# The DSA indexer of a decoder step, written out: keys of four batches turned before their products, products issued over four column strips, the sums one chunk later, all key copies on VectorE, and ScalarE left to issue loads

## The reference, cut to what matters

```python
s = jnp.einsum('bqhi,bki->bqhk', iq, ik)                              # iq: 8 x 8 tokens, 4 heads, 64 wide; ik: 8 x 4104 keys, 64 wide
score = jnp.einsum('bqhk,bqh->bqk', jax.nn.relu(s), iw)               # a weighted sum of 4 heads
score = jnp.where(causal[None], score, -jnp.inf)
vals, idx = lax.top_k(score, top)                                     # 256 keys for each query, taken later
```

## Time and profile before

| what | value |
|---|---|
| time, median of 3 runs | 3029.92 us (3025.42 to 3032.97) |
| the profiled execution, its own time | 3023.38 us |
| its span, first to last instruction | 3021.5 us |
| the stage of `index_scores`, first load to last instruction | 1377.2 to 1516.1 us |
| one chunk of the stage, from the fourth on | 15.12 us |
| granted TensorE clock over the span | 0.907 |

### The profile page before, as it was taken

One profiled execution on the slowest core, in us unless ns is written; L12 is line 12 of the kernel. 1 busy time (PEld: TensorE's weight loads), 2 busy tenths in 40 slices (PEclk: granted clock), 3 DMA queues, 4 the chain that ended last, 5 costly groups with the idle time before them and its releaser, 6 DMA issues. The chain is left out here.

```text
span 3021.5 us, 45203 instructions
## 1 busy us (share of the span) xinstructions
PE 2406.0 (80%) x16080; PEld 1792.4 (59%) x16080; DVE 1041.9 (34%) x1834; ACT 757.9 (25%) x1700; POOL 494.9 (16%) x338
## 2 busy tenths in 40 slices
PE   4799999999948888836858868888499453677996
PEld 2688888888838888832335534444255342555885
DVE  3211111010002221302248846766233259655413
ACT  2000000000012222210135434454255253344000
POOL 4533333333240000000000000000000000132431
PEclk9999999999979999967979978989799775898998
DMA  2523233232376363672289889999699460001323
GB/s 82 171 99 115 99 108 105 100 114 85 150 204 216 124 209 114 213 176 64 48 264 354 298 319 381 377 375 333 198 380 340 154 215 0 1 1 69 99 84 111
DMA packets 306803, 524.96 MB, mean 174 GB/s; under 512 B 63373, under 2 KB 80030, under 8 KB 304174
## 3 DMA queue, kind: packets, MB, share of 16 engines
q1 hardware_dynamic: 272442, 486.57, 47.2%
q10 hardware_dynamic: 31648, 31.64, 3.5%
q0 software_dynamic: 2560, 4.80, 0.5%
HBM read 500.65 MB, written 44.00 MB: 180 GB/s over the span
## 5 line engine op out<-in xcount | busy, mean ns | idle before, releaser
L422 PE MATMUL proj_acc<-proj_w_hi,h_hi 128*128 128x512 f32 (+1 forms) x960 | 370.0, 385 | 16.6 <-POOL proj_w_lo L391 16.6
L423 PE MATMUL proj_acc<-proj_w_hi,h_lo 128*128 128x512 f32 (+1 forms) x960 | 370.1, 386 | 0.0
L424 PE MATMUL proj_acc<-proj_w_lo,h_hi 128*128 128x512 f32 (+1 forms) x960 | 369.6, 385 | 0.0
L391 POOL TENSOR_TENSOR proj_w_lo<-proj_w,proj_w_hi 128x2048 fp32r<-128x2048 f32 (+1 forms) x60 | 272.0, 4534 | 476.2 <-DVE proj_w_hi L360 476.2
L360 DVE CAST proj_w_hi<-proj_w 128x2048 fp32r<-128x2048 f32 (+1 forms) x60 | 80.6, 1345 | 483.6 <-PE proj_acc L415 461.8
L664 PE MATMUL cmp_hp<-cmp_xT,cmp_w 128*128 128x128 f32 x2048 | 230.0, 275 | 0.0
L664 PEld LDWEIGHTS cmp_hp<-cmp_xT,cmp_w 128*128 128x128 f32 x2048 | 229.3, 192 | 0.0
L1186 PE MATMUL sb_tp<-kept_consts,sb_k_rows 128*128 128x128 f32 x1024 | 170.0, 316 | 64.1 <-DMA sb_k_rows<-in_cache_sb_kv_dram 47.1
L422 PEld LDWEIGHTS proj_acc<-proj_w_hi,h_hi 128*128 128x128 f32 x960 | 180.8, 188 | 52.7 <-issue 17.1
L446 ACT COPY proj_out<-proj_acc 128x512 f32<-128x512 f32 (+1 forms) x60 | 34.7, 579 | 705.6 <-PE proj_acc L424 705.6
L1186 PEld LDWEIGHTS sb_tp<-kept_consts,sb_k_rows 128*128 128x128 f32 x1024 | 127.2, 159 | 138.6 <-ACT sb_kT L1326 63.7
(11 more groups left out here) (398 smaller groups left out, 3599.7 us busy)
## 6 DMA issues: line engine op xcount, KB each, us to landing
cmp_rows<-in_cache_nsa_kv_dram SPq DMA_DIRECT2D x256, 256.0 KB, 5.2
slc_rows<-in_cache_nsa_kv_dram SPq DMA_DIRECT2D x256, 256.0 KB, 5.0
sb_k_rows<-in_cache_sb_kv_dram SPq DMA_DIRECT2D x256, 256.0 KB, 5.9
sb_v_rows<-in_cache_sb_kv_dram SPq DMA_DIRECT2D x256, 256.0 KB, 7.3
dsa_rows<-in_cache_dsa_kv_dram SPq DMA_DIRECT2D x256, 256.0 KB, 4.9
proj_w<-in_w_in_dram SPq DMA_DIRECT2D x56, 1024.0 KB
fin_w<-in_w_out_dram SPq DMA_DIRECT2D x32, 512.0 KB
proj<-proj_out ACTq DMA_DIRECT2D x14, 1024.0 KB, 4.4
```

The lines of the kernel that those rows point to most:

```text
L391: pool.tensor_tensor(w_lo[q][:, :, 0:width], w[q][:, :, 0:width], w_hi[q][:, :, 0:width], ALU.subtract).then_inc(lo_made, 1)
L422: pe.matmul(to, h_hi[:, kk, r], w_hi[q][:, k, 0:width], start=(kk == 0), stop=False)
L423: pe.matmul(to, h_lo[:, kk, r], w_hi[q][:, k, 0:width], start=False, stop=False)
L424: last = pe.matmul(to, h_hi[:, kk, r], w_lo[q][:, k, 0:width], start=False, stop=(kk == KT_IN - 1))
```

## The change

Only `index_scores` is changed. Its arithmetic is the same.

- Three sets of `rows` instead of two (BUF), four `tp` instead of two (TB), eight `kT` (one for each batch) instead of two.
- PE: the keys of batches 0 to 3 are turned, then the sums of the chunk before are taken, then batches 4 and 5 are turned, then the products of batches 0 to 3 are issued, then 6 and 7 are turned, then the products of 4 to 7. Within a group the first half of all four strips comes ahead of the second half. One semaphore increment for four products.
- DVE makes all eight key copies of a chunk. It weighs group 0 after them, and group 1 after the first two copies of the next chunk.
- ACT issues the loads of a chunk, and from the fourth chunk on copies the `total` of three chunks before behind them.
- All loops are written out.

```diff
-        rows = [s.sb(f"rows{i}", [P, NB, PPC, 64]) for i in range(2)]
-        kT = [s.sb(f"kT{i}", [P, 2, P]) for i in range(2)]
+        BUF, TB = 3, 4
+        rows = [s.sb(f"rows{i}", [P, NB, PPC, 64]) for i in range(BUF)]
+        kT = [s.sb(f"kT{b}", [P, 2, P]) for b in range(NB)]
-        tp = [s.ps(f"tp{i}", [P, 2, P]) for i in range(2)]
+        tp = [s.ps(f"tp{i}", [P, 2, P]) for i in range(TB)]
...
+        def load(eng, engine, first, c):
+
+            pages = page_numbers(nc, io, kept.by_chunk, (c * NB + first) * PPC, 4 * PPC, engine)
+            for b in range(first, first + 4):
+                if c >= BUF:
+                    eng.wait_ge(turned, (c - BUF) * NB + b + 1)
+                load_pages(eng, pages[(b - first) * PPC:(b - first + 1) * PPC], rows[c % BUF][:, b], io.idx_cache, 0, 64, rows_in[c % BUF][b])
 
         @block.sync
         def _(sp):
...
+            for c in range(NCH):
+                load(sp, mybir.EngineType.SP, 0, c)
 
         @block.tensor
         def _(pe):
...
+            def turn(c, b):
+                n = c * NB + b
+                pe.wait_ge(rows_in[c % BUF][b], 64 * (c // BUF) + 64)
+                if n >= TB:
+
+                    pe.wait_ge(copied, n - TB + 1)
+                for q in range(2):
+                    last = pe.transpose(tp[n % TB][:, q, :], rows[c % BUF][:, b, 2 * q:2 * q + 2, :].rearrange("p a d -> p (a d)"), kept.ident)
+                last.then_inc(turned, 1)
+
+            def products(c, g):
+                if c:
+                    pe.wait_ge(weighted, (c - 1) * 2 + g + 1)
+                pe.wait_ge(copied, c * NB + 4 * g + 4)
                 for half in range(2):
-                    to = sp_[g][32 * r:32 * r + 32, :].rearrange("p (q a k) -> p a q k", a=2, k=P)[:, half]
-                    last = pe.matmul(to, kept.q_idx[:, half, b, :], kT[b % 2][:], start=(half == 0), stop=(half == 1),
-                                     tile_position=(0, 32 * r), skip_group_check=True)
+                    for r in range(4):
+                        to = sp_[g][32 * r:32 * r + 32, :].rearrange("p (q a k) -> p a q k", a=2, k=P)[:, half]
+                        last = pe.matmul(to, kept.q_idx[:, half, 4 * g + r, :], kT[4 * g + r][:], start=(half == 0), stop=(half == 1),
+                                         tile_position=(0, 32 * r), skip_group_check=True)
                 last.then_inc(multiplied, 1)
...
+            def add_up(c, width):
+                if c:
+                    pe.wait_ge(total_copied, c)
+                for g in range(2):
+                    pe.wait_ge(weighted, c * 2 + g + 1)
+                    pe.matmul(total[:, 0:width], seli[g], relu[g][:, 0:width], start=(g == 0), stop=(g == 1)).then_inc(summed, 1)
+
+            for c in range(NCH):
+                for b in range(4):
+                    turn(c, b)
+                if c:
+                    add_up(c - 1, CH)
+                for b in range(4, 6):
+                    turn(c, b)
+                products(c, 0)
+                for b in range(6, NB):
+                    turn(c, b)
+                products(c, 1)
+            add_up(NCH - 1, CH)
...
         @block.vector
         def _(dve):
...
+            def copy_keys(c, b):
+                dve.wait_ge(turned, c * NB + b + 1)
+                if c:
+
+                    dve.wait_ge(multiplied, (c - 1) * 2 + b // 4 + 1)
+                dve.tensor_copy(kT[b][:], tp[(c * NB + b) % TB][:]).then_inc(copied, 1)
+
+            def weigh(c, g, width):
+                dve.wait_ge(multiplied, c * 2 + g + 1)
+                if c:
+                    dve.wait_ge(summed, (c - 1) * 2 + g + 1)
...
+            for c in range(NCH):
                 for b in range(NB):
-                    if b % 2 == 0:
-                        copy_keys(dve, c * NB + b, b)
-                    if b == 5:
-                        weigh(0, c, CH)
-                weigh(1, c, CH)
...
+                    copy_keys(c, b)
+                    if b == 1 and c:
+                        weigh(c - 1, 1, CH)
+                weigh(c, 0, CH)
+            weigh(NCH - 1, 1, CH)
+            weigh(NCH, 0, NT)
+            weigh(NCH, 1, NT)
...
         @block.scalar
         def _(act):
...
+            def take_total(c):
+                act.wait_ge(summed, c * 2 + 2)
+                act.copy(kept.scores[:, c * CH:(c + 1) * CH], total[:]).then_inc(total_copied, 1)
+
+            for c in range(NCH):
+                load(act, mybir.EngineType.Activation, 4, c)
+                if c >= BUF:
+                    take_total(c - BUF)
+            for c in range(NCH - BUF, NCH):
+                take_total(c)
```

More of the change, by code:

```diff
@@ L823, in index_scores @@
         sp_ = [s.ps(f"sc{g}", [P, CH]) for g in range(2)]
         total = s.ps("total", [NS, CH])
-        rows_in = [[s.sem(f"rows_in{i}_{b}") for b in range(NB)] for i in range(2)]
-        turned, even_copied, odd_copied, multiplied = s.sem("turned"), s.sem("even_copied"), s.sem("odd_copied"), s.sem("multiplied")
+        rows_in = [[s.sem(f"rows_in{i}_{b}") for b in range(NB)] for i in range(BUF)]
+        turned, copied, multiplied = s.sem("turned"), s.sem("copied"), s.sem("multiplied")
         weighted, summed, total_copied, masked = s.sem("weighted"), s.sem("summed"), s.sem("total_copied"), s.sem("masked")
-        copied_by = (even_copied, odd_copied)
@@ L842, in _ @@
         @block.sync
         def _(sp):
[L844 to L848, removed]
+            for c in range(NCH):
+                load(sp, mybir.EngineType.SP, 0, c)
         @block.tensor
         def _(pe):
-            pe.nop().then_inc(turned, 2 * NB)
-            pe.nop().then_inc(multiplied, 2)
@@ L855, in product @@
-            def product(b, n):
-                g, r = divmod(b, 4)
-                pe.wait_ge(copied_by[b % 2], n + 2)
+            def turn(c, b):
[6 more added lines that the diff above has]
+                last.then_inc(turned, 1)
@@ L895, in _ @@
+            add_up(NCH - 1, CH)
             for g in range(2):
-                pe.wait_ge(weighted, NCH * 2 + g + 1)
+                pe.wait_ge(weighted, (NCH - 1) * 2 + g + 1)
                 for r in range(4):
@@ L900, in _ @@
                                      start=True, stop=True, tile_position=(0, 32 * r))
[L901 to L912, removed]
+                last.then_inc(multiplied, 1)
@@ L914, in _ @@
+            add_up(NCH, NT)
         @block.vector
         def _(dve):
[L916 to L922, removed]
+            def copy_keys(c, b):
[3 more added lines that the diff above has]
+                dve.tensor_copy(kT[b][:], tp[(c * NB + b) % TB][:]).then_inc(copied, 1)
@@ L923, in weigh @@
+            def weigh(c, g, width):
+                dve.wait_ge(multiplied, c * 2 + g + 1)
+                if c:
+                    dve.wait_ge(summed, (c - 1) * 2 + g + 1)
                 dve.tensor_scalar(relu[g][:, 0:width], sp_[g][:, 0:width], 0.0, kept.w_idx[:, g:g + 1], ALU.max, ALU.mult).then_inc(weighted, 1)
-            with dve.Fori(0, NCH) as c:
+            for c in range(NCH):
                 for b in range(NB):
-                    if b % 2 == 0:
-                        copy_keys(dve, c * NB + b, b)
-                    if b == 5:
-                        weigh(0, c, CH)
-                weigh(1, c, CH)
@@ L932, in _ @@
-            weigh(0, NCH, NT)
-            weigh(1, NCH, NT)
-            dve.wait_ge(summed, 2 * NCH + 2 + 2)
+                    copy_keys(c, b)
[5 more added lines that the diff above has]
+            weigh(NCH, 1, NT)
+            dve.wait_ge(summed, 2 * NCH + 2)
             dve.tensor_tensor(kept.scores[:, PAST:KEYS], total[:, 0:NT], kept.consts[0:NS, C_NM:C_NM + NT], ALU.add).then_inc(masked, 1)
```

## The result

The changed kernel takes 2985.68 us (median of 4 runs, 2982.61 to 2989.57) against 3028.54 for the kernel before in the same measurement (4 runs). The ratio is 0.986, 95% interval 0.9847 to 0.9874, a gain of 42.9 us. A second measurement on another occasion gave 0.9865 (0.9843 to 0.9887). The forecast was 2984.

What follows compares the result with a forecast made beforehand. PE's order of work bounded most of the stage; after the change, load issues would. Issues ending at 1453.1 plus a 16.8 us end gave 1469.9 instead of 1516.1, so 3029.9 - 46 = 2984 us, range 2976 to 3004.

Steps and rivals of the forecast that it cites:

- The place: The `index_scores` stage overlaps neither neighbour, so its shortening from 138.9 us, 46.2 us, reaches the kernel's total whole.
- The sign that would have spoken against it: The next stage, `slc_sample`, lengthening after its earlier start; it was forecast to keep its length.
- PE's chunk: PE's work per chunk in `index_scores` falls from 15.1 to 7.0 us, with four products overlapping on four strips.
- the wait for the last copy: PE's second product group waits 0.6 us a chunk for DVE's key copy of batch 7.
- The loads as the bound: SP's and ACT's load issues, 9.5 us a chunk, exceed PE's 7.0 and set the stage's pace.
- The term for irregular issues: Extra time in the load lists: chunk 0's 0.4 us excess over chunk 1, put down three more times.
- The end: From the last load issue to the stage's end, 16.8 us, as PE waits for totals ACT copies behind loads.
- DVE: Eight copies and two weighings, 4.9 us a chunk, 7 with semaphores; expected under 6 us busy, not the bound.
- the slack: PE's spare time under the load issues, about 2.5 us in each 9.5 us chunk.
- rival 1: PE stays the bound through a lower clock or non-overlapping strips: 12.7 us a chunk, gain 23, 3007 us; chance 0.15.
- Rival 3: Transfers in 256-byte packets can't keep the rate; at 57 GB/s the stage is 25 us longer, 3055 us; chance 0.04.
- Rival 2: Load issues slow to 0.8 us each, 14.0 us a chunk; total within 0.3% of before; chance 0.04.

Runs made afterwards that it cites:

- x1_serial: Changed kernel, but in a group of four products both halves of a strip are issued before the next strip's; stage 93.9 us.
- x3_one_issue: Changed kernel, four page transfers replaced by one of the same bytes from neighbouring pages, page numbers not read; stage 63.7 us.
- x5_pool: As x2_early, with loads split over three queues (SP 3 batches, ACT 3, GpSimd 2); stage 69.8 us, 2948.58 us, ratio 0.9747 to the kernel before.
- x2_early: Changed kernel, with ACT's copy of a total two chunks behind its loads instead of three; stage 90.4 us, median 2977.97 us.
- x4_act_copies: Changed kernel, but ACT copies the odd batches' keys between its load issues and takes the total one chunk later instead of three; stage 101.3 us.
- a_again: The changed kernel once more, unchanged; stage 92.9 us, 2981.44 us median of 5 runs.

## Why the prediction was right, point by point

**The place.** The stage is closed, and its 45.6 us reached the total but for noise: the medians moved by 42.9, with an interval of 38 to 46. The changed kernel's profiled execution took 6.7 us more outside the stage than that of before, which is within the spread given above. That the total came within 2 us of the forecast is luck for that reason; the stage, 92.7 us forecast and 93.3 measured, is the fairer test. The sign that would have spoken against it didn't appear: from the first to the last of its page loads `slc_sample` took 201.6 us before, and 203.0 and 201.8 us in the two executions of the changed kernel.

**PE's chunk.** 7.0 us forecast, 6.85 measured; the group 1.05 against 1.07; the wait for the last copy 0.6 against 0.72. That the group would overlap was read rightly from the earlier trace rows. Interleaving the halves was not needed for it (x1_serial).

**The loads as the bound.** The end of the last issue was forecast 75.9 us after the first, from ACT's list. ACT's last issue ends at 76.6 us, and SP's at 77.1. (The terms as written add up to 1452.9 and not 1453.1.) x3_one_issue and x5_pool show the bound from both sides: fewer issues, or more issuers, and the stage falls to 64 and 70 us. Two errors nearly cancel in the sum. The term for irregular issues was too small: 0.4 us three times were put down, and ACT had three issues of 0.9 to 1.4 us and one of 0.7, together 2.9 us over the usual. A chunk without one took 9.3 us, less than the 9.5 put down. The pace came to 9.9 us in chunks 4 to 7.

**The end.** 16.8 us forecast from the last issue, 16.6 measured from ACT's copy at 1458.65 to the end. Here too two terms cancel: PE's work up to its last full add-up took 10.9 us instead of 10.4, and the rest 3.3 instead of 3.8. Its cause, the total copied behind the loads, is confirmed in the rows. But the prediction put the end some 8 us shorter without it, and x2_early gained 2.9: the rows' landing and the clock took its place.

**DVE.** Under 6 us a chunk forecast; 35.3 us in the four windows above, 4.4 a chunk. The Trainium skill, page "TensorEngine Tiling (Array Packing)", section "Performance Considerations", advises both ScalarE and VectorE for the PSUM copies. In the one arrangement of this that was run, x4_act_copies, the stage was 8 us longer, since ScalarE is also an issuer of loads here.

**The rivals.** PE's clock did fall once more after it had risen, while PE stood for the total of chunk 0. The windows, and PE's row behind the gap:

```profile
1407.60:1414.40 6.80, 4.25 (x47) 2.28 (x45) 4.24 (x10) 0.00 (x0) 0.00 (x0) 1.00 0.49 109
1414.40:1424.60 10.20, 4.15 (x7) 1.29 (x8) 0.00 (x0) 0.58 (x1) 0.00 (x0) 0.50 0.50 111
...
1420.45 3.67 PE L874 MATMUL idx_total<-idx_relu,kept_consts 128*64 128x512 f32 x4 [7.60 <-ACT scores L930]
```

The add-up behind the gap took 3.67 us instead of 1.93, and the wait for the total in the next chunk was only 0.91 us: the slack hid it. From 1424.6 to 1475.3 the clock was 1.00. So rival 1 was there and cost next to nothing. Rival 3 falls with x3_one_issue: 219 GB/s is reached in these pieces. Rival 2, a slower issue, is there in small: the issues over the usual cost 2.9 us, where 1.2 had been put down.

## What to carry to other kernels

When one engine's chunk is cut in half, add up what its old length was covering: here 256 load issues of about 0.5 us each, spread over two queues, which then set the pace. Look closely before you ask an engine that issues transfers in order to wait for others between them. A small result that it copies behind its loads ties the engine that needs the copy to the loads. After this change the next gain was in the number of issuers, not in the matmuls.

## What the runs showed of the hardware

**Slow load issues lie at fetches of instruction code.** In the changed kernel one SP issue takes 1.38 us instead of 0.33, and one of ACT at the same moment 1.40. The transfers between 1393.0 and 1394.2 hold a 16 KB fetch of code (timeline of SP, and transfers by queue):

```profile
1393.66 1.38 SPq L559 DMA_DIRECT2D idx_rows<-in_cache_dsa_idx_dram  x1
```

```profile
q8 instruction: 1, 0.02, 6.4%
```

The other slow issues of about 1 us (46.7 and 61.5 us after the first) and those of x2_early and x5_pool lie at such fetches too. Where the fetch lies elsewhere, the slow issue does too: the second of them is 39.8 us after the first issue in x1_serial, with its fetch at 39.5, instead of 46.7 and 46.2. To test whether the fetches are the cause I put code on GpSimd, which is idle in this stage.

```diff
+        @block.gpsimd
+        def _(pool):
+            for n in range(1024):
+                pool.nop().then_inc(filler, 1)
```

x9_pool_nops had the same without the increment. 

> The changed kernel with 1024 do-nothing instructions on GpSimd, idle in this stage otherwise; nothing else waits for them. Theory A (fetches of instruction code hold up the load issues: in the trace of the changed kernel the slow issues of about 1 us lie at the same times as 16 KB fetches of the instruction queue): the added code brings 4 or more further fetches in the stage, each with a slow issue on both queues, and the stage grows from 93 to 96 or more. Theory B (the coincidence is one of time only): more fetches, no more slow issues, 93 us.

Its instructions were not in the trace and the fetches were the changed kernel's, so it is one more repetition, with 93.6 us.

> The do-nothing instructions of the run before left no trace on GpSimd, so they were not in the program. Here each of 1024 increments a semaphore that nobody waits for. Theory A (instruction fetches hold up the load issues): several further fetches in the stage, each with slow issues of about 1 us on both load queues, and a stage of 96 us or more. Theory B (a coincidence of time only): further fetches without further slow issues, 93 to 94 us.

Transfers by queue in the stage, first of the changed kernel, then of this one:

```profile
q8 instruction: 4, 0.07, 0.3%
q14 instruction: 7, 0.06, 0.2%
```

```profile
q14 instruction: 15, 0.12, 0.5%
q8 instruction: 4, 0.07, 0.3%
```

There are eight more fetches of 8 KB. At three, 21.5, 28.0 and 52.5 us after the first issue, both queues had an issue of 0.53 to 0.69 us, and at two more one queue had (0.74 and 0.51). The two at 21.5 and 52.5 have no counterpart in the changed kernel; the one at 28.0 has one, at 28.6, without a slow issue. SP's timeline shows the first:

```profile
1401.02 0.65 SPq L559 DMA_DIRECT2D idx_rows<-in_cache_dsa_idx_dram  x1
```

The last issue came 1.8 us later than in the changed kernel and the stage was 3.5 us longer, 96.8. The other 1.7 us are the clock's: it was 0.51 from 1458.6 to 1462.1, and the add-up there took 3.63 us instead of 1.93.

```profile
1458.58 3.63 PE L880 MATMUL idx_total<-idx_relu,kept_consts 128*64 128x512 f32 x4 [2.37 <-ACT scores L936]
```

So the added code did bring slow issues where there had been none, but fewer and shorter ones than theory A had it, and the stage passed theory A's 96 us only by the clock. Of the 1.8 us, little is certain: among four executions with the same load lists and without the added code (the changed kernel, a_again, x1_serial, x9_pool_nops) SP's last issue moved by 1.2 us, and it came 1.0 us after the latest of them. That a fetch makes an issue slow is likely from these runs but not shown, and GpSimd's 1024 increments, which ran all through the stage, are not told apart from its code. By the same count the kernel before had 6 fetches in the stage and the changed one 11. The written-out loops are the likely reason; no run changes them alone. The four slow issues of ACT in the changed kernel add 2.9 us to its list, which is an upper bound for their price.

**An issue can take long for the transfers before it.** A 32 KB page is 0.33 us of issue, or 0.52 with its register work. A transfer of four pages, in 512 pieces, took 0.51 us at the end of SP's list and 1.17 in its middle, at 219 GB/s (x3_one_issue). That the 1.17 us are a wait for the transfers before, and not the price of the pieces, fits this, but isn't tested apart.

**GpSimd issues page loads nearly as fast as SP.** An issue is 0.534 us against 0.333 on SP, but 8 take 4.61 us, 0.58 each with the register work, against 0.52 on SP. Landing takes 2.7 us against 2.4 on SP (x5_pool).
